# First block of a fused two-block network: the step-size projection computed with its weights held in four column groups, and channel tiles turned two groups behind

## The chip, the cores and the metric

The kernel runs on one core of a Trainium2 chip. The metric is the device time of one execution in microseconds (us), lower is better. The core has a matrix engine (TensorE, PE in the profile, with its weight loads as PEld), three engines for elementwise work (VectorE or DVE, ScalarE or ACT, GpSimd or POOL), and an engine that here only issues transfers (SyncE or SP). Each runs its own instruction stream in order and waits for the others on semaphores.

## The reference

Two network blocks run one after the other on 512 tokens of width 1024. The first block has a state-space mixer, a long convolution and a product-key expert layer; the second has recurrent mixers and feed-forward layers. The change lies in the input side of the state-space mixer:

```
p_l = modulate(rmsnorm(h_lat, norm1[i]), sh1_l, sc1_l) @ w_in[i]      # 512 tokens
p_c = modulate(rmsnorm(h_ctx, norm1[i]), sh1_c, sc1_c) @ w_in[i]      # 256 context tokens
...
xbc = jax.nn.silu(dwconv_centred(proj[..., OFF_XBC:OFF_DT], conv_w, conv_b))
dt_raw = proj[..., OFF_DT:OFF_HY]                                    # 32 columns: 16 heads, two directions
dt_f = jax.nn.softplus(dt_raw[..., :SSD_HEADS] + dt_bias[0])...
```

So for 768 tokens a projection to 2048 channels (16 tiles of 128), a centred convolution of width 5 over time and a silu, and beside it a projection of the same 1024 inputs to only 32 columns, the step sizes `dt`.

## The kernel before

Everything is in float32. A large product is made of three products of rounded parts (`fp32r`): each weight unit of 128x1024 is loaded by SP (`load`), rounded by ACT (`hi`, line 236), and its remainder is taken by DVE (`lo`, line 242). Three such pairs of buffers (`RW = 3`) go round in a ring: ACT may round unit u only when PE has used unit u-3. Small products run in plain float32, where one product shows in the profile as two records of PE.

Weights stream in one fixed order, and each stage is written out by hand for each engine. The stage of the change is `conv` (`conv_s`, `conv_t`, `conv_v`, `conv_a`, `conv_g`), which begins once the normalised inputs stand in SBUF: `CHX` (eight tiles of 128 channels x 512 tokens) and `BTOK` (eight of 128x256, the context).

- PE (`conv_t`): the first two channel tiles ("groups" 0 and 1) are projected together: 48 products of 512 columns (lines 806 to 808), then for the same 512 tokens the `dt` products (line 818), then 48 products of 256 columns for the context and the `dt` products of the context. After them `totok_t(0)` turns the finished tile 0 (six transposes, line 284), and a loop over groups 2 to 15 computes each group of 24 products of 512 columns (and up to group 11 another 24 of 256), followed by `totok_t(o - 1)`. Ahead of group 14 stand the cumulated sums of the step sizes (`cumsum`, line 831, and `total`, line 833).
- DVE (`conv_v`): for each tile o the remainder of the weight unit three groups on, the convolution in five instructions (one at line 901, four at line 904), then `totok_v(o - 1)`, the copies of the turned tile from PSUM (lines 869 and 870). In tiles 3, 4 and 5 it also works off pieces of the softplus of `dt`.
- ACT (`conv_a`): for each tile o the rounding of the unit three groups on (line 236), which waits for the use of unit o, then the copies of the projected tile out of PSUM (`conv in`, lines 933 and 935), then after the convolution its silu (`conv out`, lines 940 and 942). After tile 1 it begins the softplus.

The bank rules tie these together: group o waits for `conv in` of o-2, `totok_t(o)` for the copies of tile o-2, and

```
            if o == 14:
                t.wait_ge(*S.at("aa"))
                t.wait_ge(*S.at("tok", 10))
```

that is, the sums wait until DVE has copied the turned tile 10 out of the banks that they write. The stage after `conv`, `states`, runs products (line 996) against what POOL and DVE make of its tokens.

A product in column groups is in the kernel before too: `modmm_t` (line 603) holds 128x32 weights, streams 512 columns, and writes the parts of the sum over k to the PSUM partitions 0, 32, 64 and 96, by `32 * (k % 4)`.

Of the kernel before, what the change touches and what calls it, by code (L numbers as in the profile page):

```python
# [65 lines left out]
class Area:  # L66
# [11 lines left out]
    ("rk_ka", 4), ("rk_rk", 4), ("rk_lg", 4), ("rk_lb", 4), ("gla_gb", 2), ("gla_norm", 4),  # L78
]
CST_COLS = [("ident", 128), ("ones", 128), ("bd64", 128), ("triF", 128), ("triB", 128), ("mask2", 512),  # L80
            ("lev", 384), ("strict", 64), ("eye64", 64), ("reset", 512), ("iota128", 128), ("iota16", 16), ("one1", 1), ("fold", 2)]


def layout(cols):
# [21 lines left out]
class Program:  # L106
# [504 lines left out]
    def modtr_t(self, t, n, b):  # L611
        S, L = self.S, self.L1
        t.wait_ge(*S.at("modrow", n))
        for o in range(4):
            m = t.matmul(self.PS[b][:, 2 * o:2 * o + 2], self.v(L.ROW + 512 * (n % 2) + 128 * o, 128), self.cst("fold"), start=True, stop=True)
        m.then_inc(*S.on("t", "modtr", n))

    def modrow_v(self, v, n, b):
# [173 lines left out]
    def conv_t(self, t):  # L792
        S, L, PS = self.S, self.L1, self.PS
        u0 = self.cur["t"] // 8
        self.cur["t"] += 16
        xn, ctx = self.pair(L.XN, 8), lambda k: (self.vr(L.WKB + 256 * k, 256), self.vr(L.XDF + 2048 + 256 * k, 256))
        for rhs, name, b, n in ((xn, "x", 0, 512), (ctx, "ctx", 2, 256)):
            for k in range(8):
                t.wait_ge(*S.at("nlo", name, k))
                for i in range(2):  # L800
                    at = self.wr0 + 2048 * ((u0 + i) % RW)
                    hi, lo = (self.vr(at + x, 1024)[:, 128 * k:128 * k + 128] for x in (0, 1024))
                    if k == 0:
                        t.wait_ge(*S.at("lo", u0 + i))
                    xh, xl = rhs(k)
                    t.matmul(PS[b + i][:, 0:n], hi, xh, start=k == 0, stop=False)
                    t.matmul(PS[b + i][:, 0:n], hi, xl, start=False, stop=False)
                    m = t.matmul(PS[b + i][:, 0:n], lo, xh, start=False, stop=k == 7)
                    if k == 7 and b == 2:
                        m.then_inc(*S.on("t", "used", u0 + i))  # L810
                        S.mark("t", "proj", i)

            t.wait_ge(*S.at("wdt"))
            t.wait_ge(*S.at("shifted", name, 7))
            for tt in range(4) if b == 0 else (4, 5):
                for k in range(8):
                    x = self.v(L.CHX + 512 * k + 128 * tt, 128) if tt < 4 else self.v(L.BTOK + 256 * k + 128 * (tt - 4), 128)
                    m = t.matmul(PS[7][:, 32 * tt:32 * tt + 32], x, self.v(L.WDT + 32 * k, 32), start=k == 0, stop=k == 7)
        m.then_inc(*S.on("t", "dt"))
        self.totok_t(t, 0)  # L820
        for o in range(2, 16):
            outs, rhss = [PS[o % 2][:, 0:512]], [xn]
            if o < 12:
                outs, rhss = outs + [PS[2 + o % 2][:, 0:256]], rhss + [ctx]
# [3 lines that stand above are left out]
                for c in range(6):  # L828
                    for d, tri in ((0, "triF"), (1, "triB")):
                        at = 32 * c + 16 * d  # L830
                        m = t.matmul(PS[4][:, at:at + 16], self.cst(tri), self.v(L.AA + at, 16), start=True, stop=True)
                m.then_inc(*S.on("t", "cumsum"))
                t.matmul(PS[5][:, 0:192], self.cst("ones"), self.v(L.AA, 192), start=True, stop=True).then_inc(*S.on("t", "total"))
            t.wait_ge(*S.at("conv in", o - 2))
            self.group(t, outs, rhss, 8, "proj", o)
            if o <= 12:
                self.totok_t(t, o - 1)
        self.end("t", "conv")

    def conv_tiles(self, o):  # L840
# [31 lines left out]
    def conv_v(self, v):  # L872
        S, L, PS = self.S, self.L1, self.PS
# [5 lines left out]
                v.memset(self.v(PB + 776 * i + at, m), 0.0).then_inc(*S.on("v"))  # L879
        v.wait_ge(*S.last("v"))  # L880
        d3 = self.v(L.DT, 192).rearrange("p (c h) -> p c h", c=6)
        for o in range(16):
            if o != 14:
                self.weights_v(v, 8)
# [12 lines left out]
            pb, ab, n = PB + 776 * (o % 2), AB + 772 * (o % 2), 772 if o < 12 else 512  # L897
# [6 lines left out]
                v.scalar_tensor_tensor(out=self.v(ab, n), in0=self.v(pb + j, n), scalar=self.prm("ssd_cw", 16 * j + o), in1=self.v(ab, n),  # L904
                                       op0=ALU.mult, op1=ALU.add).then_inc(*S.on("v"))
            S.mark("v", "conv", o)
            if 1 <= o <= 12:
                self.totok_v(v, o - 1)
            if o == 1:
                v.wait_ge(*S.at("dt"))  # L910
                v.tensor_tensor(d3, PS[7][:, 0:192].rearrange("p (c h) -> p c h", c=6), row6(self.prm("dt_bias", 0, 32)), ALU.add).then_inc(*S.on("v", "dt biased"))
# [9 lines left out]
    def conv_a(self, a):  # L921
        S, L, PS = self.S, self.L1, self.PS
# [3 lines left out]
        for o in range(16):  # L926
# [8 lines left out]
                a.activation(self.v(pb + 518, 256), PS[2 + o % 2][:, 0:256], ACT.Copy).then_inc(*S.on("a"))  # L935
            S.mark("a", "conv in", o)
            if o == 0:
                a.wait_ge(*S.at("dt"))
            a.wait_ge(*S.at("conv", o))
            a.activation(self.v(dl, 512), self.v(ab, 512), ACT.Silu).then_inc(*S.on("a"))  # L940
            if o < 12:
# [3557 lines left out]
def constants():  # L4499
    f = np.float32  # L4500
    p, q = np.arange(128)[:, None], np.arange(128)[None, :]
    same = (p // 64) == (q // 64)
    out = {"ident": p == q, "ones": np.ones((128, 128)), "bd64": same, "triF": p <= q, "triB": p >= q}
# [7 lines left out]
    out["iota128"] = np.broadcast_to(q, (128, 128))  # L4511
    out["iota16"] = np.broadcast_to(np.arange(16)[None], (128, 16))
    out["one1"] = np.ones((128, 1))
    out["fold"] = (p % 32) == np.arange(2)[None, :]
    cst = np.concatenate([np.asarray(out[n], f).reshape(128, m) for n, m in CST_COLS], 1)

    t, i = np.arange(512), np.arange(256)
# [99 lines left out]
```

## Time and profile before

| | |
|---|---|
| median of 3 runs | 4421.56 us (4417.78 to 4422.22) |
| the profiled execution: its time | 4415.04 us |
| the profiled execution: its span | 4413.2 us |
| PE busy | 4239.3 us (96%) |
| DVE busy | 2987.0 us (68%) |
| ACT busy | 1805.9 us (41%) |
| chain that ended last | PE 80%, DVE 10%, ACT 3%, issue 3% |

The span is the profiled execution from its first to its last instruction; 1.8 us lie around it. The busy shares are means over stages with different limits. The `conv` stage fills the stretch from 63 to 215 us, 3% of the span, so the question is what bounds it there and whether what it gains or loses reaches the end.

### The profile page before, as it was taken

To read this page: it belongs to the slowest core of one execution; us is meant where nothing else is said; L and a number is where in the kernel's file an instruction comes from. 1 tells how busy PE (TensorE), PEld (TensorE's weight loads), DVE (VectorE), ACT (ScalarE), POOL (GpSimd) and SP (SyncE) were. 2 spreads that over 40 slices of the span, in tenths; PEclk is the share of its full clock that TensorE was granted. 3 is DMA by queue.
4 is the path that set the end of the run, shared out by engine and by line. 5 is a ranking of instruction groups with operands and counts; after the bars stand their busy time and mean duration, and the time that the engine had idled before them with its cause. 6 is when DMAs were issued, how large, how long until landed. Compare 5 with 4: busy or idle time off the path is not lost.

```text
span 4413.2 us, 66804 instructions
## 1 busy us (share of the span) xinstructions
PE 4239.3 (96%) x26227; PEld 3698.9 (84%) x26227; DVE 2987.0 (68%) x5041; ACT 1805.9 (41%) x2815; POOL 1417.9 (32%) x992
## 2 busy tenths in 40 slices
PE   7978999999999999999999999999999999999998
PEld 5856755779999999999989877699889877877997
DVE  5866657559767977777678445588378545655873
ACT  4245511233335643333355345455255334324542
POOL 2044224314886545666511110212111110112121
PEclk8989999999999999999999999899999999999999
DMA  4133521224887899999733322133323232102332
GB/s 182 52 107 120 184 75 50 91 90 136 283 268 269 327 369 358 368 364 369 281 98 102 97 78 72 39 109 97 101 91 106 91 108 77 45 35 67 106 100 73
DMA packets 232192, 665.76 MB, mean 151 GB/s; under 512 B 22519, under 2 KB 88455, under 8 KB 229704
## 3 DMA queue, kind: packets, MB, share of 16 engines
q1 hardware_dynamic: 110528, 389.87, 26.4%
q0 software_dynamic: 38752, 142.90, 8.9%
q10 hardware_dynamic: 82600, 128.71, 8.2%
q8 instruction: 210, 3.44, 0.3%
q14 instruction: 102, 0.84, 0.1%
HBM read 593.24 MB, written 68.16 MB: 150 GB/s over the span
## 4 chain that ended last, share of the span: by engine, by line
PE 80%; DVE 10%; ACT 3%; issue 3%; POOL 2%; DMA 2%; ACTq 0%; DVEq 0%; POOLq 0%
PE ps L273 15%; PE ps L274 15%; PE ps L275 15%; PE ps L2732 5%; PE ps L2734 5%; PE ps L2733 5%; PE ps L1613 2%; PE ps L2326 2%; PE ps L3767 2%; PE ps L1692 1%; DMA A<-in_w_late 1%; DVE r L242 1%; DVE A L904 1%; DVE r L292 1%; PE ps L405 1%
## 5 line engine op out<-in xcount | busy, mean ns | idle before, releaser
L273 PE MATMUL ps<-r,r 128*128 128x384 f32 (+1 forms) x3944 | 1453.9, 369 | 11.8 <-POOL r L242 6.7
L274 PE MATMUL ps<-r,r 128*128 128x384 f32 (+1 forms) x3944 | 1433.8, 364 | 0.0
L275 PE MATMUL ps<-r,r 128*128 128x384 f32 (+1 forms) x3944 | 1433.3, 363 | 0.0
L242 DVE TENSOR_TENSOR r<-A,r 128x1024 fp32r<-128x1024 f32 x401 | 507.5, 1268 | 773.3 <-ACT r L236 773.1
L236 ACT ACTIVATE r<-A 128x1024 fp32r<-128x1024 f32 x513 | 542.2, 1058 | 1187.6 <-PE ps L275 1037.1
L273 PEld LDWEIGHTS ps<-r,r 128*128 128x128 f32 x3944 | 744.3, 189 | 105.2 <-issue 14.1
L274 PEld LDWEIGHTS ps<-r,r 128*128 128x128 f32 x3944 | 744.4, 189 | 81.5 <-issue 3.5
L275 PEld LDWEIGHTS ps<-r,r 128*128 128x128 f32 x3944 | 744.1, 189 | 81.2
L289 ACT ACTIVATE r<-A 128x512 fp32r<-128x512 f32 (+1 forms) x796 | 474.2, 611 | 489.7 <-DVE A L2418 223.5
L2732 PE MATMUL ps<-r,r 128*128 128x256 f32 x2128 | 601.0, 282 | 3.4 <-DVE A L2896 2.5
L2734 PE MATMUL ps<-r,r 128*128 128x256 f32 x2128 | 600.4, 282 | 0.0
L2733 PE MATMUL ps<-r,r 128*128 128x256 f32 x2128 | 599.8, 282 | 0.0
L292 POOL TENSOR_TENSOR r<-A,r 128x384 fp32r<-128x384 f32 (+2 forms) x243 | 338.7, 1401 | 618.5 <-ACT r L289 483.2
L292 DVE TENSOR_TENSOR r<-A,r 128x512 fp32r<-128x512 f32 x617 | 448.8, 742 | 10.5 <-ACT r L289 6.8
L2732 PEld LDWEIGHTS ps<-r,r 128*128 128x128 f32 x2128 | 403.7, 190 | 5.2 <-DVE A L2896 3.3
L2733 PEld LDWEIGHTS ps<-r,r 128*128 128x128 f32 x2128 | 403.8, 190 | 0.2
L2734 PEld LDWEIGHTS ps<-r,r 128*128 128x128 f32 x2128 | 403.8, 190 | 0.0
L242 POOL TENSOR_TENSOR r<-A,r 128x1024 fp32r<-128x1024 f32 x112 | 281.9, 2518 | 240.2 <-ACT r L236 239.4
L2914 POOL TENSOR_TENSOR A<-A 128x512 f32<-128x512 f32 x72 | 120.8, 1677 | 694.9 <-DVE A L2905 694.9
L2984 DVE TENSOR_TENSOR A<-A 128x512 f32<-128x512 f32 x304 | 208.1, 684 | 3.8 <-issue 0.9
L2061 DVE SCALAR_TENSOR_TENSOR A<-A 128x1024 f32<-128x1024 f32 x127 | 173.7, 1368 | 2.1
L2036 POOL DMA_INDIRECT A<-in_v_rows,A x128 | 159.1, 1243 | 22.4 <-issue 14.3
(534 smaller groups left out, 5393.6 us busy)
## 6 DMA issues: line engine op xcount, KB each, us to landing
A<-in_pu SPq DMA_DIRECT2D x128, 512.0 KB, 4.4
A<-in_pv SPq DMA_DIRECT2D x128, 512.0 KB, 6.3
A<-in_f1i SPq DMA_DIRECT2D x88, 512.0 KB, 3.5
A<-in_f2i SPq DMA_DIRECT2D x88, 512.0 KB, 3.6
A<-in_w_in SPq DMA_DIRECT2D x48, 512.0 KB, 3.7
acts<-A ACTq DMA_DIRECT2D x128, 192.0 KB, 4.4
gates<-A ACTq DMA_DIRECT2D x8, 3072.0 KB, 12.2
A<-gates ACTq DMA_DIRECT2D x32, 768.0 KB, 8.7
```

Of the source, the lines that this page charges most:

```text
L236: a.activation(self.vr(self.wr0 + 2048 * (u % RW), 1024), self.v(self.st0 + 1024 * (u % RS), 1024), ACT.Copy).then_inc(*self.S.on("a", "hi ...
L242: e.tensor_tensor(self.vr(at + 1024, 1024), self.v(self.st0 + 1024 * (u % RS), 1024), self.vr(at, 1024).bitcast(F32), ALU.subtract).then_i ...
L273: t.matmul(o, hi, xh, start=first and k == k0, stop=False)
L274: t.matmul(o, hi, xl, start=False, stop=False)
L275: m = t.matmul(o, lo, xh, start=False, stop=final and k == K - 1)
L289: a.activation(self.vr(at, n), src, ACT.Copy).then_inc(*self.S.on("a", *key))
L292: e.tensor_tensor(self.vr(lo, n), src, self.vr(at, n).bitcast(F32), ALU.subtract).then_inc(*self.S.on(who, *key))
L2061: v.scalar_tensor_tensor(out=acc, in0=row, scalar=w, in1=acc, op0=ALU.mult, op1=ALU.add).then_inc(*S.on("v", "row used", n))
L2732: t.matmul(ps[:, 0:256], hi, xh, start=opens and k == 0, stop=False, skip_group_check=not opens)
L2733: t.matmul(ps[:, 0:256], hi, xl, start=False, stop=False, skip_group_check=not opens)
L2734: m = t.matmul(ps[:, 0:256], lo, xh, start=False, stop=k == 3, skip_group_check=not opens)
L2984: v.tensor_tensor(self.operand(i, p, x), self.v(one, 512), self.v(two, 512), how).then_inc(*S.on("v", "sum", i, p, x))
```

## The change

The `dt` products are made the other way round. Before, 128 tokens of a k-tile are the held operand and the 32 columns of the weights stream past them: 48 products of 32 columns, each with a load of 128 columns. After, the 32 columns of the weights of k-tile k are held in column group k % 4 and all 512 tokens (256 of the context) stream past: 8 products of 512 columns and 8 of 256. That leaves four partial sums on four blocks of 32 partitions, with heads on partitions. DVE copies them into SBUF (`CHC`, not used until tile 12), and six products against a constant of 32 columns (`fold`, 1 where the partition mod 32 is the column) sum the four parts and turn them to tokens on partitions, into the same place of PSUM bank 7 as before.

These six products stand after group 2. `totok_t` and `totok_v` move: tile o-2 is turned after group o, where it was o-1. ACT, which waited for `dt` before the first silu, now waits for the context's parts.

```
-            for tt in range(4) if b == 0 else (4, 5):
-                for k in range(8):
-                    x = self.v(L.CHX + 512 * k + 128 * tt, 128) if tt < 4 else self.v(L.BTOK + 256 * k + 128 * (tt - 4), 128)
-                    m = t.matmul(PS[7][:, 32 * tt:32 * tt + 32], x, self.v(L.WDT + 32 * k, 32), start=k == 0, stop=k == 7)
-        m.then_inc(*S.on("t", "dt"))
-        self.totok_t(t, 0)
+            src, part = (L.CHX, PS[5][:, 0:512]) if b == 0 else (L.BTOK, PS[6][:, 0:256])
+            for k in range(8):
+                q = 32 * (k % 4)
+                m = t.matmul(part[q:q + 32, :], self.v(L.WDT + 32 * k, 32), self.v(src + n * k, n), start=k < 4, stop=k >= 4)
+                if k >= 4:
+                    m.then_inc(*S.on("t"))
+            S.mark("t", "dt parts", name)
         for o in range(2, 16):
...
             self.group(t, outs, rhss, 8, "proj", o)
-            if o <= 12:
-                self.totok_t(t, o - 1)
+            if o == 2:
+                t.wait_ge(*S.at("dt parts out"))
+                for tt in range(6):
+                    m = t.matmul(PS[7][:, 32 * tt:32 * tt + 32], self.v(L.CHC + 128 * tt, 128), self.cst("fold"), start=True, stop=True)
+                m.then_inc(*S.on("t", "dt"))
+            if o <= 13:
+                self.totok_t(t, o - 2)
...
         d3 = self.v(L.DT, 192).rearrange("p (c h) -> p c h", c=6)
+        v.wait_ge(*S.at("dt parts", "x"))
+        v.tensor_copy(self.v(L.CHC, 512), PS[5][:, 0:512]).then_inc(*S.on("v"))
...
-            if 1 <= o <= 12:
-                self.totok_v(v, o - 1)
+            if o == 0:
+                v.wait_ge(*S.at("dt parts", "ctx"))
+                v.tensor_copy(self.v(L.CHC + 512, 256), PS[6][:, 0:256]).then_inc(*S.on("v", "dt parts out"))
+            if 2 <= o <= 13:
+                self.totok_v(v, o - 2)
...
             if o == 0:
-                a.wait_ge(*S.at("dt"))
+                a.wait_ge(*S.at("dt parts", "ctx"))
```

The constant `fold` grows from 2 to 32 columns; its other user, `modtr_t`, takes the first two.

On PE, at the end of the context's part of groups 0 and 1, where the next group begins (line numbers of the changed kernel for its own rows):

```order
 L808 MATMUL ps<-r_84,r_55 128x256
-L818 MATMUL ps<-A 128x32 x16
-L284 MATMUL ps<-A 128x128 x6
+L818 MATMUL ps<-A 32x256 x8
 L273 MATMUL ps<-r_52,r_86 128x512
 L274 MATMUL ps<-r_53,r_86 128x512
```

The sixteen narrow products are eight in column groups, and the six transposes of tile 0 no longer stand between them and group 2; they come after it, behind the six `fold` products.

On PE, between the end of group 13 and the sums ahead of group 14:

```order
 L274 MATMUL ps<-r_69,r_54 128x512
 L275 MATMUL ps<-r_68,r_55 128x512
-L831 MATMUL ps<-A 128x16 x12
-L833 MATMUL ps<-A 128x192
+L284 MATMUL ps<-A 128x128 x6
+L832 MATMUL ps<-A 128x16 x12
+L834 MATMUL ps<-A 128x192
 L273 MATMUL ps<-r_52,r_86 128x512
```

The transposes of tile 11 have moved here from behind group 12; the sums follow them.

On DVE, the first three tiles of the changed kernel's convolution:

```order
L889 COPY A<-ps 128x512
L242 TENSOR_TENSOR r_51<-A,r_50 128x1024
L909 TENSOR_SCALAR A<-A 128x772
L912 SCALAR_TENSOR_TENSOR A<-A 128x772 x4
L917 COPY A<-ps 128x256
L242 TENSOR_TENSOR r_55<-A,r_54 128x1024
...
L922 TENSOR_TENSOR A<-ps,A 128x192
L242 TENSOR_TENSOR r_87<-A,r_86 128x1024
```

Before, this began at the first `L242`, had nothing between tile 0's convolution and the next `L242`, and had the two copies of a turned tile ahead of the `dt` bias (`L922` here, `L911` before); the first turned tile is now copied after tile 2's convolution.

## Rows read from the trace of the kernel before

**Rows 1.** Timeline of PE, 63 to 90 us: start, length, instruction, idle before.
```profile
63.66 8.63 PE L818 MATMUL ps<-A 128*128 128x32 f32 x64
...
76.07 0.28 PE L806 MATMUL ps<-r,r 128*128 128x256 f32 x1
...
79.51 0.28 PE L808 MATMUL ps<-r,r 128*128 128x256 f32 x1
79.63 3.92 PE L818 MATMUL ps<-A 128*128 128x32 f32 x32
89.13 1.54 PE L284 MATMUL ps<-A 128*128 128x128 f32 x6 [5.58 <-ACT A L942]
```

**Rows 2.** Timeline of PE, 28 to 37 us: one plain product, six in column groups.
```profile
31.74 1.12 PE L655 MATMUL ps<-A 128*128 128x512 f32 x2
...
34.91 1.91 PE L603 MATMUL ps<-A 128*32 128x512 f32 x12
```

**Rows 3.** Windows: stretch, length, busy PE, PEld, DVE, ACT, POOL, PEclk, DMA share, GB/s.
```profile
35.00:37.00 2.00, 1.82 (x12) 0.29 (x12) 1.99 (x2) 0.00 (x0) 0.00 (x0) 1.00 0.04 16
67.00:68.00 1.00, 1.00 (x11) 1.00 (x10) 0.00 (x0) 0.60 (x2) 0.79 (x2) 1.00 1.02 406
70.00:71.00 1.00, 1.00 (x6) 1.00 (x7) 0.00 (x0) 0.00 (x0) 0.00 (x0) 0.50 0.62 242
```

**Rows 4.** Timeline of POOL, 60 to 69 us.
```profile
60.18 6.41 POOL L292 TENSOR_TENSOR r<-A,r 128x512 fp32r<-128x512 f32 x7 [2.81 <-ACT A L695]
...
67.71 0.72 POOL L292 TENSOR_TENSOR r<-A,r 128x256 fp32r<-128x256 f32 x1 [0.21 <-ACT A L701]
```

**Rows 5.** Timeline of ACT, 79 to 101 us.
```profile
79.55 1.06 ACT L236 ACTIVATE r<-A 128x1024 fp32r<-128x1024 f32 x1 [11.92 <-PE ps L808]
...
97.34 0.36 ACT L544 ACTIVATE A<-A 128x192 f32<-128x192 f32 x1 [0.26 <-DVE A L911]
...
99.01 0.36 ACT L546 ACTIVATE A<-A 128x192 f32<-128x192 f32 x1
100.37 1.06 ACT L236 ACTIVATE r<-A 128x1024 fp32r<-128x1024 f32 x1 [0.99 <-PE ps L275]
```

**Rows 6.** Timeline of DVE: the remainders that begin tiles 0, 1, 2, 3, 6, 7, 12, and the last copy of a turned tile.
```profile
80.71 1.23 DVE L242 TENSOR_TENSOR r<-A,r 128x1024 fp32r<-128x1024 f32 x1 [11.50 <-ACT r L236]
...
90.05 1.23 DVE L242 TENSOR_TENSOR r<-A,r 128x1024 fp32r<-128x1024 f32 x1 [3.29 <-ACT r L236]
...
101.46 1.23 DVE L242 TENSOR_TENSOR r<-A,r 128x1024 fp32r<-128x1024 f32 x1 [4.16 <-ACT r L236]
...
110.53 1.23 DVE L242 TENSOR_TENSOR r<-A,r 128x1024 fp32r<-128x1024 f32 x1 [2.09 <-ACT r L236]
...
140.31 1.22 DVE L242 TENSOR_TENSOR r<-A,r 128x1024 fp32r<-128x1024 f32 x1
...
148.30 1.22 DVE L242 TENSOR_TENSOR r<-A,r 128x1024 fp32r<-128x1024 f32 x1 [0.54 <-ACT r L236]
...
193.23 1.23 DVE L242 TENSOR_TENSOR r<-A,r 128x1024 fp32r<-128x1024 f32 x1 [1.02 <-ACT r L236]
...
198.58 0.41 DVE L870 COPY A<-ps 128x256 f32<-128x256 f32 x1
```

**Rows 7.** Timeline of PE, 109 to 217 us.
```profile
109.18 0.82 PE L284 MATMUL ps<-A 128*128 128x128 f32 x6
...
192.39 0.85 PE L284 MATMUL ps<-A 128*128 128x128 f32 x6 [2.12 <-ACT A L942]
...
198.65 2.75 PE L831 MATMUL ps<-A 128*128 128x16 f32 x24
...
215.21 1.99 PE L996 MATMUL ps<-A 128*128 128x256 f32 x8 [0.69 <-ACT A L933]
```

**Rows 8.** Windows over a pause of PE in the stage after, columns as in rows 3.
```profile
226.00:230.00 4.00, 0.00 (x0) 0.00 (x0) 3.76 (x5) 4.00 (x18) 0.85 (x1) 0.95 0.40 131
230.00:232.00 2.00, 1.63 (x2) 0.18 (x2) 1.00 (x2) 2.00 (x10) 0.00 (x0) 0.50 0.00 0
```

More of the change, by code:

```diff
@@ L80 @@
 CST_COLS = [("ident", 128), ("ones", 128), ("bd64", 128), ("triF", 128), ("triB", 128), ("mask2", 512),
-            ("lev", 384), ("strict", 64), ("eye64", 64), ("reset", 512), ("iota128", 128), ("iota16", 16), ("one1", 1), ("fold", 2)]
+            ("lev", 384), ("strict", 64), ("eye64", 64), ("reset", 512), ("iota128", 128), ("iota16", 16), ("one1", 1), ("fold", 32)]
 def layout(cols):
@@ L614, in modtr_t @@
         for o in range(4):
-            m = t.matmul(self.PS[b][:, 2 * o:2 * o + 2], self.v(L.ROW + 512 * (n % 2) + 128 * o, 128), self.cst("fold"), start=True, stop=True)
+            m = t.matmul(self.PS[b][:, 2 * o:2 * o + 2], self.v(L.ROW + 512 * (n % 2) + 128 * o, 128), self.cst("fold", 0, 2), start=True, stop=True)
         m.then_inc(*S.on("t", "modtr", n))
@@ L4513, in constants @@
     out["one1"] = np.ones((128, 1))
-    out["fold"] = (p % 32) == np.arange(2)[None, :]
+    out["fold"] = (p % 32) == np.arange(32)[None, :]
     cst = np.concatenate([np.asarray(out[n], f).reshape(128, m) for n, m in CST_COLS], 1)
```

## The prediction, made before the changed kernel had run

> **What bounds the kernel now.** The page says PE 96% busy, which tells nothing about this change: what counts is the stretch from 63 to 215 us. I read the timeline of PE there first. At 63.66 us the 32 step-size products of the tokens begin and take 8.6 us, at 79.63 the 16 of the context take another 3.9, and then PE stands idle for 5.58 us until ACT's silu of tile 0 releases the transposes at 89.13 [rows 1]. So at the start of the stage PE is the bound, and it spends 12.5 us on products of almost no arithmetic.
>
> Next, the waits of ACT and DVE. ACT waited 11.92 us for PE before its first rounding, and DVE 11.50 behind it [rows 5, 6]: the whole convolution starts when PE has finished the projection of groups 0 and 1. After that there are two loops. PE needs 9.07 us for a group and its six transposes. DVE and ACT need, for one tile, the remainder of a weight unit, the convolution, the silu and the next rounding. Which one leads is seen in the starts of DVE's tiles [rows 6]: tile 2 to tile 3 takes 9.07 us, and ahead of the rounding ACT waits 0.99 us for PE [rows 5]; there PE leads. Tile 6 to tile 7 takes 7.99 us: that is the loop of DVE and ACT by itself, where PE had been held up and was no releaser. Tiles 3 to 6 take 29.78 us for three, since DVE also does the softplus; there DVE leads. From tile 7 to tile 12 it is 44.93 us for five, 9.0 in the mean: PE leads again. At the end group 12 has no context part, and PE waits 2.12 us for the silu of tile 11 before it can turn it [rows 7].
>
> **The change, part by part.**
>
> *Products of the tokens.* I have two prices for a column-grouped product, both at full length of 512. Line 603 does six in 1.91 us [rows 2]. Six are four and two, two rounds over the four column groups; the eight new ones are four and four, also two rounds, so 1.91 us. The granted clock of that stretch was 1.00 [rows 3].
>
> *Products of the context's groups 0 and 1.* They follow at once. In the trace of before they began at half clock: the narrow products ran at 11 records a us at clock 1.00, and from 70 us at 6 or 7 (6 products and 7 weight loads are counted) at clock 0.50 [rows 3]. With 512 columns streaming I take the full clock, since the same form kept it [rows 3]. Then 48 products of 256 columns cost 48 x 0.1186 = 5.69 us, where 0.1186 is (79.51 - 76.07)/29, the mean gap of the last 30 [rows 1]. Their inputs come from POOL, which is done at 68.43 us, six by 66.6 [rows 4]; PE would reach the eighth at about 70.5, so that POOL doesn't hold it. The projection ends at 63.66 + 1.91 + 5.69 = 71.26 us, where it ended at 79.63: **8.37 us earlier**. DVE's copy of the parts (0.7 us by its copies of that size) falls in its long wait and costs nothing.
>
> *Products of the context.* Two rounds of half the length, about 1.1 us (estimate from the 1.91), while ACT rounds and copies tile 0 out. Group 2 needs that copy (73.0 us), and no longer stands behind 3.9 us of products and 5.58 us of wait.
>
> *The loop of DVE and ACT.* Tile 0 begins on DVE at 80.71 - 8.37 = 72.34, tile 1 at 81.68. The `dt` bias no longer has the two copies of a turned tile ahead of it, so ACT's 0.26 us of wait before the softplus goes [rows 5]. ACT is through with it at 99.37 - 8.37 - 0.26 = 90.74. There it used to wait 0.99 us more for the end of group 2, which now comes at 81.5. Tile 2 follows the rounding by 1.09 (101.46 - 100.37): 91.83. Tile 3: 7.99 later instead of 9.07, 99.82. Tiles 3 to 6 as before, 29.78: 129.60. Tiles 6 to 12: six times 7.99, 177.54, where it was 193.23. This rests on PE being ahead: with 9.07 us a group, from 73.0 us, and 1.2 us for the `fold` products (12 records at the narrow rate), I get waits of 0.3 us twice (groups 4 and 9 for the copy of tile 2 and 7), and the end of group 13 with the transposes of tile 11 at about 178.0 us.
>
> *The sums ahead of group 14.* They wait for DVE's copy of turned tile 10. Before, that copy stood in DVE's tile 11, now it stands in tile 12. The copies there end 5.76 us after the tile's start (198.58 + 0.41 - 193.23 [rows 6]): 177.54 + 5.76 = 183.30. The sums began at 198.65 [rows 7], so **15.35 us earlier**, of which 8.37 is the start, 1.3 the softplus and its wait, and the rest the seven tiles that run at 7.99 us. But PE, done at 178.0, stands idle for 5.3 us: a new wait which did not exist.
>
> *What that wait does to the clock.* In a pause of 4.5 us in the next stage the granted clock fell from 1.00, and the first products after it ran at 0.50 [rows 8]. I take it that the clock is at half here as well. The 24 records of the sums took 2.75 us [rows 7]; narrow records cost 0.09 us at full clock and 0.154 (1/6.5) at half [rows 3], so 24 x 0.063 = 1.5 us more. Group 14 began at half clock before too, so I add nothing, with up to 1.7 us (its share of that, if it lasts once more as long) as the upper bound. Nothing at all is the lower.
>
> The Trainium skill (TensorE: Matmul & The Clock Gate, "Why this matters for your kernels") also speaks against this part of the change: it warns that a pause between bursts of products puts the clock back. The trace has it, 0.50 after 4.5 us.
>
> The same page (Part 3, "Measured speedup vs the span model") measured 2.38 times for three column groups, 0.79 of the ideal. By that, four would give 3.2 times; eight products of about 0.9 us one after the other would become 2.2 us rather than 1.9, and the sum would be 0.3 us smaller. Line 603 is the same form on this chip, so I keep its 1.91.
>
> *Downstream.* PE begins the next stage at 215.21, released by the copy of tile 15 [rows 7]; groups 14 and 15 and that copy keep their length. POOL's first product there waits for what DVE makes of the sums, and comes earlier alike. The weights' loads wait for buffers that DVE or PE frees, so they move along. I find nothing that is tied to absolute time, so the shift should reach the end.
>
> **Sum:** -15.35 + 1.5 = -13.9 us. On the profiled execution that is 4415.04 - 13.9 = 4401.1. That execution lies 6.5 us under the median of the runs shown; on the median it is 4421.56 - 13.9 = 4407.7 us. A measurement of this kernel tells about 0.2% (8.8 us) from no change, so the gain would be just visible.
>
> **The rivals.**
>
> *The clock survives the pause* (0.10): -15.4, 4406.2 us. For it: it needs only that the clock falls later than I think; against: 5.3 us is longer than the pause in rows 8.
>
> *The loop stays at PE's pace* (0.11). If the rounding or the copies out of PSUM still wait for PE's groups, seven tiles cost 9.07 instead of 7.99: 7.6 us of the gain go, -13.9 + 7.6 = -6.3, 4415.3 us. For it: 9.0 us is what tiles 7 to 12 show. Against: the wait seen was for the end of a group that now ends a whole group earlier.
>
> *The column groups run one after another* (0.04). A plain product of 512 columns is 1.12 us alone, about 0.9 in a row; eight are 7.3, 5.4 more than 1.91: -8.5, 4413.1 us. Against: six in 1.91 us.
>
> *The gain is given back downstream* (0.09): 0, 4421.6 us, if a transfer or POOL holds the start of the next stage. Against: PE was released there by ACT, not by these.
>
> *Slower* (0.04). The place is the same wait ahead of group 14. Turning one tile later makes the sums, the decay factors and so the whole next stage hang on DVE's tile 12. If the loop of DVE and ACT slows down with the new order (its reads of PSUM against PE's writes, say), the sums come later than at 198.65 once a tile takes more than 10.1 us in the mean from tile 2 to 12, where I have 8.6 and before had 9.2; at 11.0 us it is 8.8 us slower, 4430 us. Nothing in the profile shows such a cost.
>
> **How the numbers follow.** The likeliest case has 0.62 and 4407.7 us, in itself from 4405 to 4410. The range must reach to the slower pace of the loop and, downward, to the surviving clock and the scatter of a few us between runs: 4403 to 4417. Faster than 0.2%: 0.62 + 0.10 and parts of the two middle rivals, 0.76. Within 0.2%: 0.20. Slower: 0.04.
>
> **What would show it.** Right: the new products (token form) within 2 us and the context's projection ending near 71.3 us, clock 1.00 from 63 to 80; DVE's tiles 7 to 12 starting 8.0 us apart; an idle of PE of about 5 us before the sums at about 183, released by DVE's copy; the first product of the next stage near 201.3. Wrong: a clock of 0.50 in the context's projection, tiles still 9.1 us apart, or a stage after that takes longer than before by what was gained.

## The result

The changed kernel takes **4381.67 us** (median of 3 runs, 4375.46 to 4388.7) against 4421.56 before: a ratio of 0.992, with a 95% interval of 0.9901 to 0.9938. That is 40 us by the medians, where 13.9 were forecast; the time lies under the range of 4403 to 4417. A later session on one chip repeats it: 0.9908 (0.9893 to 0.9924).

The profiled execution has a span of 4379.9 us (it was 4413.2). The page's groups of the costliest instructions show where PE got its time back: fewer busy us in the same number of the same products, all over the kernel.

```profile
L273 PE MATMUL ps<-r,r 128*128 128x384 f32 (+1 forms) x3944 | 1435.8, 364 | 14.8 <-POOL r L242 7.2
L274 PE MATMUL ps<-r,r 128*128 128x384 f32 (+1 forms) x3944 | 1418.8, 360 | 0.0
L275 PE MATMUL ps<-r,r 128*128 128x384 f32 (+1 forms) x3944 | 1418.3, 360 | 0.0
```

Before, the first of the three was 1453.9 us and 369 ns, the other two 364 and 363 ns. Groups 2 to 15 of the changed stage are 576 of these 11,832 products.

The stage itself, on the timeline of PE of the changed kernel, in the places of [rows 1] and [rows 7]. This execution came to the stage 3.0 us late (66.67 instead of 63.66), so what counts are differences.

```profile
66.67 1.92 PE L818 MATMUL ps<-A 128*32 128x512 f32 x16
...
74.47 1.07 PE L818 MATMUL ps<-A 128*32 128x256 f32 x16
...
76.17 0.50 PE L273 MATMUL ps<-r,r 128*128 128x512 f32 x1 [0.63 <-ACT A L946]
...
84.67 1.42 PE L840 MATMUL ps<-A 128*128 128x32 f32 x12
85.93 0.85 PE L284 MATMUL ps<-A 128*128 128x128 f32 x6
...
186.42 5.28 PE L832 MATMUL ps<-A 128*128 128x16 f32 x24 [5.50 <-DVE A L876]
191.54 0.99 PE L834 MATMUL ps<-A 128*128 128x192 f32 x2
...
205.30 1.99 PE L1007 MATMUL ps<-A 128*128 128x256 f32 x8 [0.69 <-ACT A L944]
```

From the start of the step-size products: the projection of groups 0 and 1 ends after 7.8 us (forecast 7.6, before 15.97), the sums begin after 119.75 (forecast 119.64, before 134.99), the next stage after 138.63 (forecast 137.7, before 151.55). DVE's tiles, in the places of [rows 6]:

```profile
75.39 1.23 DVE L242 TENSOR_TENSOR r<-A,r 128x1024 fp32r<-128x1024 f32 x1 [2.40 <-ACT r L236]
...
94.68 1.23 DVE L242 TENSOR_TENSOR r<-A,r 128x1024 fp32r<-128x1024 f32 x1 [3.62 <-ACT r L236]
...
132.47 1.22 DVE L242 TENSOR_TENSOR r<-A,r 128x1024 fp32r<-128x1024 f32 x1
...
140.48 1.23 DVE L242 TENSOR_TENSOR r<-A,r 128x1024 fp32r<-128x1024 f32 x1 [0.54 <-ACT r L236]
...
180.51 1.23 DVE L242 TENSOR_TENSOR r<-A,r 128x1024 fp32r<-128x1024 f32 x1 [1.02 <-ACT r L236]
```

Tile 12 begins 113.84 us after the step-size products; the forecast had 113.88, and tiles 7 to 12 are 8.0 us apart.

The rest of the gain lies behind the stage. Two markers in the kernel before, by line (first and last start), the expert stage between them:

```profile
L2109 PE MATMUL ps<-A x128: 270/275/348, 952.2 to 1041.5; 128*128 128x128 f32 x128
...
L2732 PE MATMUL ps<-r,r x2128: 277/283/390, 2253.9 to 4269.2; 128*128 128x256 f32 x194
```

and in the changed kernel:

```profile
L2120 PE MATMUL ps<-A x128: 270/275/348, 940.4 to 1028.2; 128*128 128x128 f32 x128
...
L2743 PE MATMUL ps<-r,r x2128: 277/283/388, 2227.5 to 4238.4; 128*128 128x256 f32 x194
```

At the first marker the changed kernel is 11.8 us ahead, at the second 26.4: 14.6 us were won in a stage that the diff doesn't touch. Another 8.8 come by 3652 us (the first product of line 3540), and 1.9 are lost again behind it. A stretch of 100 us in the second half of the expert stage, in windows with the columns of [rows 3], of before:

```profile
1740.00:1840.00 100.00, 100.00 (x572) 100.00 (x571) 77.92 (x77) 37.75 (x48) 70.73 (x53) 1.00 0.99 365
```

and of the changed kernel:

```profile
1740.00:1840.00 100.00, 100.00 (x579) 100.00 (x578) 79.07 (x78) 38.02 (x48) 71.79 (x54) 1.00 1.01 370
```

579 products instead of 572 in the same time, at the same granted clock of 1.00, with PE without a gap in both. By the distances of their starts a product of 384 columns takes 0.1733 us instead of 0.1756. (Two expectations below have 0.1727 and 0.1748: 100 us over the counts, which take in products that began ahead of the window, so both are a little low.)

### The profile page after: what moved, and what is told of

It reads as the page before. It is cut to its first block, busy times and chain, and to the rows that moved or that the text cites. A ratio compares the mean times of both kernels' runs of the same rounds, so it can differ in the third digit from the quotient of the medians.

```text
span 4379.9 us, 66702 instructions
## 1 busy us (share of the span) xinstructions
PE 4206.7 (96%) x26175; PEld 3683.5 (84%) x26175; DVE 2993.5 (68%) x5043; ACT 1805.0 (41%) x2815; POOL 1425.4 (33%) x992
## 4 chain that ended last, share of the span: by engine, by line
PE 81%; DVE 10%; issue 3%; ACT 3%; POOL 2%; DMA 1%; ACTq 0%; DVEq 0%; POOLq 0%
PE ps L273 15%; PE ps L275 15%; PE ps L274 15%; PE ps L2743 5%; PE ps L2745 5%; PE ps L2744 5%; PE ps L1624 2%; PE ps L2337 2%; PE ps L3778 1%; PE ps L1703 1%; DVE A L912 1%; DVE r L292 1%; DVE r L242 1%; DMA A<-in_w_late 1%; PE ps L405 1%
## 5 line engine op out<-in xcount | busy, mean ns | idle before, releaser
L273 PE MATMUL ps<-r,r 128*128 128x384 f32 (+1 forms) x3944 | 1435.8, 364 | 14.8 <-POOL r L242 7.2
L274 PE MATMUL ps<-r,r 128*128 128x384 f32 (+1 forms) x3944 | 1418.8, 360 | 0.0
L275 PE MATMUL ps<-r,r 128*128 128x384 f32 (+1 forms) x3944 | 1418.3, 360 | 0.0
L242 DVE TENSOR_TENSOR r<-A,r 128x1024 fp32r<-128x1024 f32 x401 | 509.0, 1271 | 728.2 <-ACT r L236 715.9
L242 POOL TENSOR_TENSOR r<-A,r 128x1024 fp32r<-128x1024 f32 x112 | 284.2, 2539 | 231.7 <-ACT r L236 230.4
## 6 DMA issues: line engine op xcount, KB each, us to landing
gates<-A ACTq DMA_DIRECT2D x8, 3072.0 KB, 11.7
```

What stands on the lines that cost most here:

```text
L242: e.tensor_tensor(self.vr(at + 1024, 1024), self.v(self.st0 + 1024 * (u % RS), 1024), self.vr(at, 1024).bitcast(F32), ALU.subtract).then_i ...
L273: t.matmul(o, hi, xh, start=first and k == k0, stop=False)
L274: t.matmul(o, hi, xl, start=False, stop=False)
L275: m = t.matmul(o, lo, xh, start=False, stop=final and k == K - 1)
```

## The experiments

I had two theories for the part behind the stage. **L**: the addresses. Widening `fold` from 2 to 32 columns makes the constants longer, and each buffer that lies behind them in SBUF moves by 128 bytes. **S**: the earlier start shifts the stages against something (the clock, a transfer). And as a rival to both, **V**: the one execution or the chip. Each kernel ran beside the kernel before on the same chip; in these sessions the median of before was 4415.6 to 4418.4 us.

### The width of the constant alone

```
-            ("iota16", 16), ("one1", 1), ("fold", 2)]
+            ("iota16", 16), ("one1", 1), ("fold", 32)]
-    out["fold"] = (p % 32) == np.arange(2)[None, :]
+    out["fold"] = (p % 32) == np.arange(32)[None, :]
```

Nobody reads the 30 new columns (`layout_only` in what follows). Expected: 

> The kernel before with nothing but the constant fold widened from 2 to 32 columns, so that every buffer behind it in SBUF lies some 30 columns further. Theory L (the addresses account for what was gained behind the changed stage): 15 to 25 us faster than the kernel before, with the expert stage running 1.2% more products in 100 us, as in the changed kernel. Rival V (that part is the execution or the chip, and follows no edit) and rival S (it follows from the shift in time): no change within 0.2%.

Measured: 4392.55 us against 4415.57, ratio 0.9946 (0.9929 to 0.9964), 23 us faster. The window of the expert stage:

```profile
1740.00:1840.00 100.00, 100.00 (x579) 100.00 (x578) 77.35 (x77) 38.12 (x48) 69.68 (x54) 1.00 1.02 375
```

Its two markers:

```profile
L2109 PE MATMUL ps<-A x128: 270/275/348, 956.0 to 1043.8; 128*128 128x128 f32 x128
...
L2732 PE MATMUL ps<-r,r x2128: 277/283/388, 2243.6 to 4250.7; 128*128 128x256 f32 x194
```

At these this kernel is 3.8 us behind and 10.3 us ahead of before: 14.1 us from that stage, as in the changed kernel, with not one instruction changed. L holds, S and V fall.

### The changed kernel again, and at the old addresses

The first is the kernel as it is. Expected: 

> The changed kernel once more, as it is. If its gain of 35 us belongs to the program (L or S), 30 to 40 us faster again. If it was the execution or the chip (V), about 14 us faster, the size of the changed stage alone.

Measured: 4375.24 us, ratio 0.9908 (0.9893 to 0.9924), 40 us. It belongs to the program.

The second takes `fold` back to 2 columns:

```
-                    m = t.matmul(PS[7][:, 32 * tt:32 * tt + 32], self.v(L.CHC + 128 * tt, 128), self.cst("fold"), start=True, stop=True)
+                    for j in range(2):
+                        m = t.matmul(PS[7][:, 32 * tt:32 * tt + 32], self.v(L.CHC + 128 * tt, 128), self.cst("eye64", 32 * j, 32), start=j == 0, stop=j == 1)
```

Expected: 

> The changed kernel with fold back at 2 columns; the parts are summed by twelve products against the two halves of the identity of 64 columns instead of six against fold, so that all addresses are those of the kernel before. Theory L: only the gain of the stage, 13 to 15 us. Rival S: all of the gain, 30 to 40 us. Rival V: like the changed kernel in the same session, whatever that is.

Measured: 4405.42 us, ratio 0.9978 (0.9966 to 0.999), 10 us, a little under the 13 to 15. The next stage begins 138.71 us after the step-size products, as in the changed kernel (138.63). The expert stage is back at its old pace:

```profile
1740.00:1840.00 100.00, 100.00 (x570) 100.00 (x569) 75.81 (x76) 37.60 (x48) 67.01 (x52) 1.00 1.00 371
```

So the diff is two changes, the stage and the addresses (23 us), and 13.9 was the forecast for the first. The stage's price by the totals is 10 us here; as the changed kernel less `layout_only` in the same session (4392.55 - 4375.24) it is 17. The markers of the stage, which scatter less, give 12 to 14 (see the account of the prediction).

### The changed kernel, started late behind the stage

```
         t.wait_ge(*S.at("conv in", 15))
+        self.warm_t(t, 5, 16)
```

Expected: 

> The changed kernel with 16 more plain products of 512 columns (0.86 us each, 13.7 us) ahead of the next stage, whose results nobody reads, so that everything behind starts at about the time at which it did before. Theory L: 13 to 14 us slower than the changed kernel, some 20 us faster than before. Rival S (the gain behind the stage follows from the earlier start): all of it goes, within 0.2% of the kernel before.

Measured: 4388.59 us, 13.4 slower than the changed kernel and 27 faster than before, 0.9942 (0.9926 to 0.9958). The products take 14.00 us in the trace. By the medians, then, what is won or lost in this stage goes through to the end, which is the other half of the downstream step of the forecast. That it goes through in full isn't shown: the 13.4 is good to some 5 us (estimate from the scatter of the two sets of six runs), and by the profiles, counted from the step-size products, 9.4 and 10.0 us of it are there at the first marker.

### The two halves of the stage's change

Column groups alone: the fold and the transposes of tile 0 ahead of group 2, and the old turning.

```
+        t.wait_ge(*S.at("dt parts out"))
+        for tt in range(6):
+            m = t.matmul(PS[7][:, 32 * tt:32 * tt + 32], self.v(L.CHC + 128 * tt, 128), self.cst("fold"), start=True, stop=True)
+        m.then_inc(*S.on("t", "dt"))
+        self.totok_t(t, 0)
         for o in range(2, 16):
...
-            if o <= 13:
-                self.totok_t(t, o - 2)
+            if o <= 12:
+                self.totok_t(t, o - 1)
```

Expected: 

> The changed kernel with the turning of the tiles as it was: the products in column groups and the fold stay, but the fold and the transposes of tile 0 stand ahead of group 2 again, and every tile is turned one group behind. Mine: the projection of groups 0 and 1 ends 8 us earlier after the start of the step-size products, as in the changed kernel; the idle of 5.6 us ahead of the transposes stays, PE paces tiles 7 to 12 at 9.1 us, and the sums come 8 to 11 us earlier. With the addresses of the changed kernel (-23 us) 30 to 34 us faster than before. Rival (the column groups bring all of the stage's gain, the turning nothing): the sums come 13 to 15 us earlier.

Measured: 4393.23 us against 4417.51, ratio 0.9937 (0.992 to 0.9955), 24 us faster with the addresses in it; I had expected 30 to 34. The profiled execution is 29.8 us ahead of before at 3652 us and loses 10.4 of it behind, a stretch that takes from 760.6 to 777.9 us in the profiles with before's own instructions, so the miss is no argument about the stage. PE still stands idle ahead of the first transposes, now in front of the fold (6.29 us). The sums begin 126.5 us after the step-size products, 8.5 earlier than before:

```profile
67.03 1.92 PE L818 MATMUL ps<-A 128*32 128x512 f32 x16
...
84.77 1.52 PE L284 MATMUL ps<-A 128*128 128x128 f32 x6
...
187.41 0.84 PE L284 MATMUL ps<-A 128*128 128x128 f32 x6 [2.25 <-ACT A L953]
193.56 2.75 PE L837 MATMUL ps<-A 128*128 128x16 f32 x24
...
209.92 1.99 PE L1007 MATMUL ps<-A 128*128 128x256 f32 x8 [0.69 <-ACT A L944]
```

The sums take 2.75 us here, and the next stage comes after 142.89 us, 8.7 earlier than before, 4.3 later than in the changed kernel. The rival, that the turning brings nothing, falls.

Turning alone, on the kernel before:

```
-        self.totok_t(t, 0)
...
-            if o <= 12:
-                self.totok_t(t, o - 1)
+            if o <= 13:
+                self.totok_t(t, o - 2)
...
-            if 1 <= o <= 12:
-                self.totok_v(v, o - 1)
+            if 2 <= o <= 13:
+                self.totok_v(v, o - 2)
```

Expected: 

> The kernel before, with its own step-size products and addresses, but every tile turned two groups behind. Mine: the start of the stage stays, the tiles from 7 to 12 run at 8.0 us, PE idles ahead of the sums, and these come 4 to 7 us earlier, 3 to 6 us on the whole. Rival: the sums come not earlier at all, since the copy of tile 10 is one tile later.

Measured: 4413.4 us, ratio 0.9989 (0.9977 to 1.0), 4 us, at the edge of the noise. The sums come after 129.77 us, 5.2 earlier than before, and wait for DVE's copy:

```profile
197.38 5.04 PE L830 MATMUL ps<-A 128*128 128x16 f32 x24 [3.38 <-DVE A L869]
...
217.25 1.99 PE L995 MATMUL ps<-A 128*128 128x256 f32 x8 [0.69 <-ACT A L932]
```

8.5 and 5.2 us make 13.7 of the 15.2 by which both together bring the sums forward. The missing 1.5 is the start of this execution: its 64 narrow records took 10.30 us where before's took 8.63 (the last section has more of that), and DVE's tile 0 began 18.73 us after the step-size products instead of 17.05:

```profile
67.61 10.30 PE L818 MATMUL ps<-A 128*128 128x32 f32 x64
...
86.34 1.23 DVE L242 TENSOR_TENSOR r<-A,r 128x1024 fp32r<-128x1024 f32 x1 [14.74 <-ACT r L236]
```

Counted from tile 0 the four kernels fall into two pairs: the sums come after 117.9 us before and 117.8 with the column groups alone, and after 111.0 both here and in the changed kernel. So the column groups bring tile 0 forward by 8.3 us, the turning brings the sums forward by 6.9, and these make the 15.2. Of the 6.9 only 3.6 reach the next stage here (130.9 us from tile 0, before 134.5); the other 3.3 are lost behind the start of the sums, which take 5.04 us instead of 2.75.

### The price of the new wait

The changed kernel with the sums in banks that are free after group 11, so that nothing waits for tile 10:

```
-                t.wait_ge(*S.at("tok", 10))
+                t.wait_ge(*S.at("conv in", 11))
...
-                        m = t.matmul(PS[4][:, at:at + 16], self.cst(tri), self.v(L.AA + at, 16), start=True, stop=True)
+                        m = t.matmul(PS[2][:, at:at + 16], self.cst(tri), self.v(L.AA + at, 16), start=True, stop=True)
...
-                t.matmul(PS[5][:, 0:192], self.cst("ones"), self.v(L.AA, 192), start=True, stop=True).then_inc(*S.on("t", "total"))
+                t.matmul(PS[3][:, 0:192], self.cst("ones"), self.v(L.AA, 192), start=True, stop=True).then_inc(*S.on("t", "total"))
```

and their readers likewise. Expected: 

> The changed kernel with the sums ahead of group 14 in banks 2 and 3, which are free after group 11, so that they don't wait for the copy of turned tile 10. If the pause of 5.5 us and the half clock behind it are what the change lost there, the next stage starts 6 to 8 us earlier than in the changed kernel. Rival: the wait only moves to DVE's tiles, under 2 us.

Measured: 4372.88 us, ratio 0.9905 (0.9884 to 0.9926); by the total this can't be told from the changed kernel's 0.9908. The trace can:

```profile
179.31 2.75 PE L832 MATMUL ps<-A 128*128 128x16 f32 x24
181.91 0.57 PE L834 MATMUL ps<-A 128*128 128x192 f32 x2
...
200.11 3.73 PE L1007 MATMUL ps<-A 128*128 128x256 f32 x8 [6.70 <-ACT A L944]
```

The sums begin 114.10 us after the step-size products (119.75 in the changed kernel), at full clock. But the next stage begins after 134.90, only 3.7 us sooner (5.0 against the second profile of the changed kernel), between my 6 to 8 and the rival's 2: PE now waits 6.70 us for DVE's and ACT's last tile and its first products run at half clock (0.53 in the window from 198 to 204 us). Part of the wait moved to where DVE is the bound. By the trace of the stage it is the best version that was run; by the total that isn't shown.

### Which addresses

Four more kernels move parts of the kernel before by some bytes; in SBUF the operand that PE streams in the expert stage lay 128 bytes behind a multiple of 256 (counted from the start of the buffer area) and the weights on multiples of 256. The stage has two halves with different streamed operands: the normalised tokens (`HN`), up to 1640 us, and the weighted activations (`AC`), from there on.

```
         L.HN = self.HR
-        self.top = L.HN + 8192
+        self.top = L.HN + 8192 + 32
```

This moves all buffers of the stage but the tokens by 128 bytes, `AC` among them (`pad_behind`). Expected: 

> The kernel before with the streamed operands of the expert stage where they were, and all its buffers behind them 128 bytes further. The mirror of the last one: no change if the streamed operand counts, about 15 us faster if the gathered rows or the other buffers do.

Its mirror has `L.HN = self.HR + 32` and again 32 columns behind, so the tokens move by 128 bytes and `AC` by 256 (`pad_operands`). Expected: 

> The kernel before with the streamed operands of the expert stage (and of no other) 128 bytes further in SBUF, and what lies behind them 256 bytes further. If what counts is the place of the operand that PE streams, modulo 256 bytes, the expert stage runs 579 products in 100 us instead of 572 and the kernel is about 15 us faster. If it is the place of the other buffers (gathered rows, gates), no change.

I had overlooked that `AC` is a streamed operand too; read with that, both show the same. The starts of PE's products over 60 us, counted by their distance (0.17 or 0.18 us as rounded in the trace):

```
                 first half (1150-1210 us)   second half (1900-1960 us)
                   0.17      0.18              0.17      0.18
before             165       131 (+35 of 0.19) 152       191
layout_only        221       112               232       115
pad_behind         137       194               231       116
pad_operands       221       115               137       205
```

Each half is fast where its own streamed operand has moved by 128 bytes, and only there. On the whole they are 0.9988 (0.9977 to 0.9998) and 0.9986 (0.9975 to 0.9996), 3 and 6 us. The next kernel (`pad_gates`) moves `GB` and `AC` by 128 bytes and neither the tokens nor the gathered rows:

```
+        self.top += 32
         L.DOT, L.COEF, L.GATE, L.IDX = (self.al(128) for _ in range(4))
```

Expected: 

> The kernel before with, in the expert stage, everything behind the gathered rows 128 bytes further, the second half's streamed operand among it; the first half's streamed operand and the gathered rows stay. Streamed operand: second half 579 products in 100 us, first half as before, some 7 us. Gathered rows: no change.

Measured: second half 579 in 100 us, first half slow (133 and 199), total 0.999 (0.9973 to 1.0008), which tells nothing. And both operands (`pad_both`). It is `pad_operands` with another 128 bytes ahead of `AC`, so the tokens move by 128 bytes and `AC` by 384, which is 128 modulo 256, and not by 128 as the expectation has it:

```
-        L.GB, L.AC, L.TM = self.al(12 * NT), self.al(32 * NT), self.HX
+        L.GB = self.al(12 * NT)
+        self.top += 32
+        L.AC, L.TM = self.al(32 * NT), self.HX
```

Expected: 

> The kernel before with, in the expert stage, the streamed operands of both halves 128 bytes further (the gathered rows and gates by 256). If these two operands are what the addresses did there, both halves run at the faster rate (fewest gaps of 0.18 us in the first, 579 products in 100 us in the second) and the kernel is some 12 us faster.

Measured: 4405.39 us against 4418.39, ratio 0.9972 (0.9955 to 0.9989), 13 us, both halves fast (218 to 109, and 231 to 116). The complement (`pad_not_expert`), the widened constant but the expert stage another 128 bytes on, is layout_only with

```
-        L.HN = self.HR
+        L.HN = self.HR + 32
```

Expected: 

> The kernel of layout_only (all 128 bytes further), but in the expert stage another 128 bytes, so that its operands lie at the old place modulo 256. If the expert stage brought 12 to 15 of the 23 us, this one is 6 to 10 us faster than before, with 570 to 572 products in 100 us there.

Measured: 4410.77 us, 0.9979 (0.9967 to 0.999), 8 us, with 570 products in 100 us. 13 and 8 make 21 of the 23.

The time between the two markers, one profile each, says it with less noise than the totals and in clean steps:

```
no half moved       before 1301.7, old_layout 1302.3, pad_not_expert 1302.4
first half          pad_operands 1295.7
second half         pad_behind 1295.3, pad_gates 1294.8
both halves         pad_both 1287.6, layout_only 1287.6, the changed kernel 1287.1
```

The 8 us outside the expert stage lie in other products that stream without a gap. A stretch of products of 512 columns near the end, of before:

```profile
4320.00:4360.00 40.00, 40.00 (x172) 32.14 (x171) 14.65 (x17) 7.42 (x7) 1.29 (x1) 1.00 0.29 92
```

and of `pad_not_expert`:

```profile
4320.00:4360.00 40.00, 40.00 (x176) 32.79 (x175) 14.04 (x18) 7.42 (x7) 2.58 (x2) 1.00 0.28 92
```

`layout_only` has 176 there too, and `pad_both`, where only the expert stage moved, 172. By the starts of the products of one group, 0.2326 us a product become 0.2271. Summed over the 4104 products of 512 columns behind the second marker it is 16.5 us in both kernels with the wider constant. The 6384 products of 256 columns there (lines 2732 to 2734) go the other way, 0.1193 to 0.1201 us, and give 5.1 back. With another 4 to 5 us from the products of 512 columns ahead of the first marker that is some 15 us (estimate), at the upper end of what the total of `pad_not_expert` allows (4 to 15). The lengths of the stretches behind the second marker don't settle it: from there to 3652 us it is 1397.9 us before and 1387.3 in `layout_only`, but 1390.7 in `pad_both` as well.

Two other distances:

```
-            ("iota16", 16), ("one1", 1), ("fold", 2)]
+            ("iota16", 16), ("one1", 1), ("fold", 18)]
```

and the same with 64 (`pad_64` and `pad_256`, by the bytes that they move). Expected of the first: 

> The kernel before with the constant fold at 18 columns, so that everything behind it lies 64 bytes further (it was 128 bytes behind a multiple of 256, is now 192). The earlier runs say that PE streams 384 columns in 0.1727 us instead of 0.1748 when the streamed operand starts at a multiple of 256 bytes (counted from the start of the buffer area). If only that multiple counts, this kernel stays at 570 to 572 products in 100 us and within 0.2% of before. If any multiple of 64 but not 128 spoils it further, it is slower; if only 128 is bad, it is as fast as layout_only, 20 us.

Measured: 1.0006 (0.9991 to 1.0021), with a slow first half (138 and 194) and a fast second (578 products). That fits none of the three: at 64 bytes more, the halves part ways. Expected at 256 bytes: 

> The same with fold at 64 columns, everything behind it 256 bytes further. By the theory of the streamed operand modulo 256 bytes: no change in the expert stage (570 to 572 products in 100 us) and none on the whole. By a theory that any move away from the old place helps, or of 512 bytes: 579, and some 20 us.

Measured: 1.0002 (0.9989 to 1.0016), both halves slow (133 and 198; 153 and 190). So the pattern repeats after 256 bytes. In the stretch near the end both kernels have 172 products, as before.

### The stream by itself

```
+        for k in range(24):
+            x, y = (self.vr(self.L1.XN + 512 * i, 512) for i in (k % 8, (k + 3) % 8))
+            t.matmul(self.PS[5][:, 0:384], x[:, w // 4:w // 4 + 128], y[:, r // 4:r // 4 + 384], start=True, stop=True)
```

ten times with other `w` and `r`, behind group 15 of the kernel before. Expected: 

> The kernel before with ten times 24 extra products behind group 15, whose results nobody reads: 128x128 weights, 384 columns, both from the normalised inputs. Only the place of the streamed operand changes from set to set: 0, 128, 64, 192, 32 and 256 bytes into its tile; then the weights 128 bytes on, with the stream at 0 and at 128; then 0 and 128 again. If the address of the stream alone decides, the sets at 0 and 256 take one time (24 x 0.1748 = 4.2 us) and those at 128 another (24 x 0.1727 = 4.14 us), and so in the repeats. If it takes writes beside it, all ten are alike.

From the starts of the 240 products, the mean distance within each set (from its second to its last), with the place of the stream less that of the weights, modulo 256 bytes:

```
set   weights, stream moved by   stream less weights   us a product
1     0, 0                       0                     0.1743
2     0, 128                     128                   0.1759
3     0, 64                      64                    0.1731
4     0, 192                     192                   0.1748
5     0, 32                      32                    0.1733
6     0, 256                     0                     0.1736
7     128, 0                     128                   0.1763
8     128, 128                   0                     0.1734
9     0, 0                       0                     0.1735
10    0, 128                     128                   0.1759
```

My expectation, that the place of the stream alone decides, is wrong in an instructive way: the same stream (moved by 0 or by 128) is fast or slow, as the weights move. The three sets with a distance of 128 bytes between the two take 0.1759 to 0.1763 us, and the sets with 0 take 0.1734 to 0.1736, but for the first (0.1743), whose opening products are uneven. At 128 the products aren't all slower: every fifth or sixth starts 0.181 to 0.183 us after the one before it, the others 0.172 to 0.177. The difference is 1.5% in the mean, near the 1.3% of the expert stage, where before the streamed operands were 128 bytes off the weights modulo 256, and after are not. At 192 the set takes 0.1748, between the two, which goes with the slow first half at 64 bytes more; the fast second half there doesn't fit, and stays open.

## Why the prediction was wrong

- *Products in column groups*: right. Forecast 1.91 and about 1.1 us, measured 1.92 and 1.07. They kept the clock; the changed kernel shows 1.00 from 69 to 74 us, where [rows 3] had 0.50 from 70:

```profile
69.00:74.00 5.00, 5.00 (x44) 5.00 (x43) 0.93 (x7) 1.61 (x4) 2.12 (x3) 1.00 0.80 320
```

- *Start of the stage*: 8.37 us forecast. From the starts it is 15.97 - 7.80 = 8.2.
- *Loop of DVE and ACT*: right within 0.1 us at tile 12. The rival that it stays at PE's pace didn't come.
- *Sums ahead of group 14*: 15.35 us forecast, 134.99 - 119.75 = 15.24 measured; PE idles 5.50 us (forecast 5.3), released by DVE's copy.
- *Price of the clock*: the mechanism was right, the term too small. The changed kernel there, windows with the columns of [rows 3]:

```profile
181.00:186.00 5.00, 0.00 (x0) 0.00 (x0) 4.86 (x8) 0.62 (x2) 0.00 (x0) 0.87 0.31 105
186.00:191.00 5.00, 4.58 (x22) 4.61 (x22) 4.61 (x8) 1.22 (x4) 0.00 (x0) 0.50 0.02 3
191.00:196.00 5.00, 5.00 (x17) 4.25 (x17) 1.66 (x5) 1.77 (x3) 1.83 (x1) 0.61 0.00 0
```

  The sums took 5.28 us where I had 2.75 + 1.5. From the sums to the next stage it is 18.88 us, 2.3 more than before (16.56), and 3.6 more in the second profile of the changed kernel, against the 1.5 forecast. Since the stage began with less clock in other executions (last section), the whole is better judged against the nine profiles that keep the old start and turning (before and eight of the kernels with moved addresses): they need 151.3 to 155.2 us from the step-size products to the next stage, 153.1 in the mean. The changed kernel's two need 138.63 and 139.88, in the mean 13.8 less. Against the one profile on which the forecast was built (151.55) it is 12.9 and 11.7. So the stage gave about what was forecast, and how near it comes to 13.9 is in part luck: the price of the clock was too small by 0.8 to 2.1 us, and the start of the stage scatters by as much.
- *Downstream*: **this is the step that failed.** "I find nothing that is tied to absolute time, so the shift should reach the end" held as far as the late start can tell (13.4 us for 14.0 by the medians). But it asked only whether the shift survives, not whether the stages behind stay as they were. The front had said that `fold` grows from 2 to 32 columns, and the sum had no term for it. Its term is 23 us, more than any other: 14 in the expert stage, where the operands that PE streams had lain 128 bytes off the weights modulo 256, and the rest in the stages around it. With it the sum would have been -13.9 - 23 = -37 us, where 40 were measured. It also wasn't among the rivals: none of them was a gain larger than 15.4.

The Trainium skill (SBUF — State Buffer, "SBUF: two separate sides") says that PE never waits on anyone at its ports. No run here sets PE against another engine there. What the runs show is that at clock 1.00 PE's own pace changes with the distance of its two operands, by 1.5% in the stream by itself; whether that is a wait at a port they don't show.

What stays open: by what mechanism the distance acts; why the second half of the expert stage is fast at 64 bytes more; and why the products of 256 columns lose by the move that those of 384 and 512 gain by. The buffers outside the expert stage weren't moved one by one, so for them the distance to the weights is argued and only the move is shown.

## What to carry to other kernels

A change that lengthens any table moves all that is allocated behind it; list it as a part of the change, and run it alone (here a constant that nobody reads, 23 of 40 us). Judge a change of one stage by the times between two markers around it, since the total mixes it with everything else. And where PE streams without a gap, try the placing of the streamed operand against the weights: it costs nothing but an offset. Measure it for each shape: here one move made products of 384 and 512 columns faster and those of 256 slower.

## What the hardware showed that I had not expected

- Products of 384 columns at clock 1.00 take 0.1733 or 0.1756 us in the kernel, 0.1735 or 0.176 by themselves, as weights and stream are 0 or 128 bytes apart modulo 256.
- The same move of 128 bytes takes products of 512 columns near the end from 0.2326 to 0.2271 us, 2.4%, and products of 256 columns from 0.1193 to 0.1201.
- Narrow records at half clock cost more than I took from [rows 3]: 24 records of 16 columns take 2.75 us at clock 1.00 and 5.28 at 0.50, 0.115 and 0.22 us each.
- Where the clock falls differs between executions of the same instructions: the 64 narrow records of [rows 1] took 8.6 us before and 9.7 in the kernel with moved tokens, which alone shifts the stage by 1.6 us:

```profile
63.85 9.69 PE L818 MATMUL ps<-A 128*128 128x32 f32 x64
81.44 3.65 PE L818 MATMUL ps<-A 128*128 128x32 f32 x32
```
